# A decoder layer with a routed MoE on one core: the first weight half ahead of the second tile of x, and the second tile turned inside the first dense unit

## What is computed

```
h    = rmsnorm(x, g_mix)             # x * rsqrt(mean(x*x) + 1e-6) * g_mix
proj = h @ w_in                      # 1024 x 3848, q, k, v of two kinds of attention
...
gates = sigmoid(h @ w_gate + b_gate)
x     = x + merged @ w_out
...
x     = x + moe_ffn(rmsnorm(x, g_ffn))   # 64 experts, top 8, and a shared one
```

## Time and profile before

| | |
|---|---|
| median of 3 runs | 1102.56 us (1102.43 to 1103.54) |
| profiled execution, its own time | 1102.48 us |
| its span in the trace | 1100.7 us |
| TensorE busy | 1081.0 us, 98% |
| VectorE busy | 882.3 us, 80% |
| ScalarE busy | 739.3 us, 67% |
| GpSimd busy | 299.2 us, 27% |
| mean granted clock of TensorE | 0.997 of full speed |

### The profile page before, as it was taken

The page is one execution under the profiler, slowest core; times in us unless marked ns, Lnnn a source line. Parts: engine busy times, 40 slices in busy tenths (PEclk is TensorE's granted clock), DMA queues, the critical chain, the costliest instruction groups (busy, mean ns, idle before and its releaser), DMA issues.

```text
span 1100.7 us, 19484 instructions
## 1 busy us (share of the span) xinstructions
PE 1081.0 (98%) x5823; PEld 892.3 (81%) x5823; DVE 882.3 (80%) x1405; ACT 739.3 (67%) x1304; POOL 299.2 (27%) x288
## 2 busy tenths in 40 slices
PE   8999999999999999999999999999999999999995
PEld 7789988877777887678888888888888888888884
DVE  6543386478865835589999999999999999999993
ACT  6434465544346521268888888888888888888883
POOL 1221021000000001125433333344434444434442
PEclk9999999999999999999999999999999999999998
DMA  7243212421522093679999999999999999999982
GB/s 250 78 116 109 83 51 66 153 77 40 138 112 97 11 380 142 251 257 371 387 391 386 375 388 381 380 371 388 383 382 384 389 381 383 382 373 386 366 271 37
DMA packets 97353, 284.71 MB, mean 259 GB/s; under 512 B 19683, under 2 KB 22251, under 8 KB 96924
## 3 DMA queue, kind: packets, MB, share of 16 engines
q1 hardware_dynamic: 78876, 250.52, 59.6%
q0 software_dynamic: 18432, 33.61, 12.5%
HBM read 279.79 MB, written 37.81 MB: 289 GB/s over the span
## 4 chain that ended last, share of the span: by engine, by line
PE 91%; DVE 5%; ACT 1%; DMA 1%; issue 1%; POOL 1%; SPq 0%; ACTq 0%; POOLq 0%
PE bank L1849 32%; PE bank L1670 23%; PE bank L1863 17%; PE bank L1877 5%; PE bank L1823 3%; PE bank L1612 3%; PE bank L1837 3%; PE bank L1857 1%; DVE w_lo L1092 1%; PE bank L1697 1%; PE bank L1726 1%; PE bank L1739 1%; PE bank L1936 1%; PE bank L1715 1%; DMA arena<-in_x 0%
## 5 line engine op out<-in xcount | busy, mean ns | idle before, releaser
L1849 PE MATMUL bank<-gu_parts,xT_parts 128*128 128x512 f32 x1280 | 338.7, 394 | 0.0
L1849 PEld LDWEIGHTS bank<-gu_parts,xT_parts 128*128 128x128 f32 x1280 | 235.4, 188 | 45.9
L1863 PE MATMUL bank<-w_lo 128*128 128x512 f32 x804 | 201.6, 399 | 0.0
L1863 PEld LDWEIGHTS bank<-w_lo 128*128 128x128 f32 x804 | 146.3, 188 | 28.5 <-issue 0.5
L605 POOL TENSOR_TENSOR turn<-minus_half 16x1 f32<-16x1 f32 x123 | 73.6, 599 | 335.0 <-DMA out<-arena,idxs 174.4
L616 POOL DMA_INDIRECT out<-arena,idxs x64 | 124.7, 1948 | 46.0 <-issue 15.0
L1670 PE MATMUL bank<-w_hi,hT_hi 128*128 128x512 f32 (+1 forms) x320 | 124.8, 390 | 1.4 <-DVE arena L1187 0.7
L1670 PE MATMUL bank<-w_hi,hT_lo 128*128 128x512 f32 (+1 forms) x320 | 121.8, 381 | 0.0
L1670 PE MATMUL bank<-w_lo,hT_hi 128*128 128x512 f32 (+1 forms) x320 | 121.6, 380 | 0.0
L1452 DVE TENSOR_TENSOR gu_parts<-arena,gu_parts 128x1024 fp32r<-128x1024 f32 x96 | 116.6, 1215 | 0.4 <-PE bank L1837 0.3
L1452 DVE TENSOR_TENSOR gu_parts<-arena_x,gu_parts 128x1024 fp32r<-128x1024 f32 x96 | 116.6, 1215 | 0.1
(11 more groups left out here) (228 smaller groups left out, 1903.9 us busy)
## 6 DMA issues: line engine op xcount, KB each, us to landing
arena<-in_w_gate_e SPq DMA_DIRECT2D x64, 512.0 KB
arena<-in_w_up_e SPq DMA_DIRECT2D x64, 512.0 KB
arena<-in_w_down_e SPq DMA_DIRECT2D x64, 512.0 KB
arena_x<-in_w_gate_e SPq DMA_DIRECT2D x64, 512.0 KB
arena_x<-in_w_up_e SPq DMA_DIRECT2D x64, 512.0 KB
arena_x<-in_w_down_e SPq DMA_DIRECT2D x64, 512.0 KB
arena<-in_w_in SPq DMA_DIRECT2D x14, 1024.0 KB, 5.6
arena<-in_w_gate SPq DMA_DIRECT2D x8, 1024.0 KB, 5.6
```

The lines of the kernel that those rows point to most:

```text
L1849: last = nc.tensor.matmul(out_, a[:, PER * c + j, :], b[c][:, :, j, :], start=(c == 0 and j == 0 and i == 0), stop=(c == CHUNKS - 1 and j ...
L1863: last = nc.tensor.matmul(psY[h][0:rows, :], midT[n][a][:, j, 0:rows], w[b][:, j, h * 512:(h + 1) * 512], start=(j == 0 and k == 0), stop= ...
```

## The change

On SP, half 0 of chunk 0 is issued ahead of tile 1 of x, half 1 behind it. On ScalarE the square of tile 1 moves behind the high parts of blocks 0 to 3. On VectorE the copies and the low part of tile 0 and residues 0 to 3 come first; the mean of tile 1 follows, then residue 4, the scaling of tile 1, residues 5 and 6, the first copy of tile 1, residue 7, the second copy and the low part. On TensorE tile 1 is turned inside unit 0, after step 5, and the warm-up behind tile 0 is 56 products in one piece in place of 35 and 14.

```
--- before.py
+++ after.py
@@ -421,8 +421,9 @@
             load_x(0)
             sp.dma_start(cst[:], consts).then_inc(const_in, 16)
             sp.dma_start(gmixT[:], g_mix.rearrange("(p j) -> p j", p=P)).then_inc(const_in, 16)
+            load_half(0, 0)
             load_x(1)
-            load_chunk(0)
+            load_half(0, 1)
             for t in range(2, NT):
                 load_x(t)
             sp.dma_start(relb[0:REL_BUCKETS, :], rel_bias).then_inc(table_in, 16)
@@ -712,9 +713,11 @@
                 nc.scalar.activation(hT_hi[:, :, cols], hT[:, :, cols], ACT.Copy).then_inc(hT_hi_ready, 1)
 
             square_x(0)
+            high_hT(0)
+            for j in range(HALF):
+                split_block(0, j)
             square_x(1)
-            high_hT(0)
-            for j in range(ND):
+            for j in range(HALF, ND):
                 split_block(0, j)
             high_hT(1)
             square_x(2)
@@ -1107,22 +1110,22 @@
                 nc.vector.tensor_scalar(xn[t % 2], xin[t], hn_r[:, t:t + 1], None, ALU.mult).then_inc(xn_ready, 1)
 
             norm_x(0)
+            dve.wait_ge(const_in, 32)
+            copy_wide(("x", 0), hT, gmixT)
+            low_hT(0)
+            for j in range(HALF):
+                split_block(0, j)
             dve.wait_ge(squared, 2)
             means[0] += 1
             nc.vector.tensor_scalar(hn_ms[:, 1:2], hn_ss[:, 1:2], 1.0 / D, EPS, ALU.mult, ALU.add).then_inc(mean_ready, 1)
-            dve.wait_ge(const_in, 32)
-            copy_wide(("x", 0), hT, gmixT)
+            split_block(0, HALF)
             dve.wait_ge(rnorm_ready, means[0])
             nc.vector.tensor_scalar(xn[1], xin[1], hn_r[:, 1:2], None, ALU.mult).then_inc(xn_ready, 1)
-            low_hT(0)
-            for j in range(HALF):
-                split_block(0, j)
+            split_block(0, HALF + 1)
+            split_block(0, HALF + 2)
             copy_wide(("x", 1), hT, gmixT, (0,))
-            for j in range(HALF, HALF + 2):
-                split_block(0, j)
+            split_block(0, HALF + 3)
             copy_wide(("x", 1), hT, gmixT, (1,))
-            for j in range(HALF + 2, ND):
-                split_block(0, j)
             low_hT(1)
             norm_x(2)
             norm_x(3)
@@ -1636,9 +1639,7 @@
                     transposes(("x", t, b), [(xn[t % 2][:, j::ND], P) for j in range(b * ND // 2, (b + 1) * ND // 2)])
 
             turn_x(0)
-            keep_warm(WARM_UP * 5 // 8)
-            turn_x(1)
-            keep_warm(WARM_UP // 4)
+            keep_warm(WARM_UP)
             def stationary_of(h, j, t, by_residue):
 
                 return h[:, j, t::NT] if by_residue else h[:, j, t * P:(t + 1) * P]
@@ -1676,6 +1677,8 @@
             def dense(n):
                 for j in range(ND):
                     dense_step(n, j)
+                    if n == 0 and j == HALF + 1:
+                        turn_x(1)
                     if n == 1 and j in (2, 6):
                         turn_x(2 + j // 4)
```

## The result

| | before | changed |
|---|---|---|
| median of 7 runs each | 1103.45 us | 1106.64 us |
| lowest and highest | 1102.43 to 1104.07 | 1106.13 to 1108.60 |
| profiled execution, its own time | 1102.48 | 1108.60 |
| its span | 1100.7 | 1106.8 |
| ratio, 95% interval | | 1.0036 (1.0026 to 1.0045) |

The change makes the kernel slower by 0.36%, 2.9 to 5.0 us by the interval. The ratio goes by the means of the runs (1103.18 and 1107.13, 3.95 apart); the medians are 3.19 apart. The direction was forecast (slower, 0.73); the time of 1105.2 and the range up to 1106.3 were too low. Two things belong to that. The shift in the opening is 3.3 and not 2.75. And 1102.48, from which the sum started, lies 0.97 under the median of 1103.45, at the low end of what the kernel before does (1101.6 to 1105.9 in all its runs of this study).

A forecast was written before the change was run, and what follows sets the result against it. VectorE's program order was taken to bound the opening, TensorE the rest. Waits of 0.67, 0.67, 0.97 and 1.25 less 0.74 gave 2.8, taken as 2.75; on 1102.48 that made 1105.2 us, range 1103.9 to 1106.3.

The forecast's parts named there:

- The start: Opening: tile 0's copies no longer wait behind tile 1's mean, so dense work starts 0.74 us earlier, at 12.35.
- The four waits: VectorE in unit 0: half 1 0.67, scaling of tile 1 0.67, transposes 0.97, high part 1.25 us.
- The third: VectorE's wait for the transposes of tile 1 before its first copy, 0.97 us.
- the fourth: VectorE's wait for tile 1's high part, before the low part, 1.25 us.
- The first wait: VectorE before residue 4: half 1 lands at 14.0 as before, a new wait of 0.67 us.
- rival D: Opening loads: half 0, tile 1 or half 1 lands late; 3.1 to 3.8 us slower, 1105.6 to 1106.3; chance 0.06.
- The base: Whole kernel: the profiled execution's 1102.48 us, 0.08 under the median of three runs, to which the shift was added.
- The end: After the opening: every microsecond of TensorE's delay comes out at the end; 2.75 us added.
- A (absorbed): VectorE's chain holds less than added, above all at hand-overs; 0.8 us goes, 1104.4; chance 0.15.
- B (not slower): Low part of tile 1 ends by 19.6, VectorE's waits covered; 1102.5 us; chance 0.05.
- C (the clock): TensorE's clock falls to 1.2 GHz in unit 1; 5.5 us more, 1110.7; chance 0.04.
- the upper end of 10.9: Half 0 of chunk 0 lands at 10.9 as before instead of 9.2; 0.3 us more at the end.

The follow-up runs named there:

- copies_together: Changed kernel with both copies of tile 1 ahead of residue 7 instead of one on each side; 1106.40 us, ratio 1.0026 to the kernel before.
- loads_back: Changed kernel with the loads in their old order (tile 1 of x, half 0, half 1); 1106.47 us, ratio 1.0033 to the kernel before.
- loads_alone: Kernel before with only the new order of loads, every engine's list as before; 1107.47 us, ratio 1.0040.
- turn_and_copies: Changed kernel with tile 1 turned after step 4 and both its copies ahead of residue 7; 1104.55 us, ratio 1.0013 to the kernel before.
- delay: Kernel before with 56 more warm-up products on TensorE behind unit 3, opening untouched; 1106.74 us, ratio 1.0038.
- after_again: Changed kernel run once more, unaltered, for a second trace; 1107.27 us, ratio 1.0034 to the kernel before.

## Why the forecast was right, and where it failed

**The start.** Forecast: copies at 7.9, high part 9.28, low part 10.37, residue 0 at 11.51, first product 12.35. Measured: 7.92, 9.30, 10.39, 11.54, 12.37. The rule of start distances held to 0.03. Half 0 was forecast at 9.2 with 10.9 as the other end; it came at 9.5 and 10.65 in the two traces of the changed kernel, and 11.2 in copies_together, outside both ends. The warm-up products ended at 11.4, ahead of the first product, and cost nothing.

**The four waits.** Forecast 0.67, 0.67, 0.97 and 1.25; measured 1.11 (VectorE's mean at 13.94 to residue 4 at 15.05), 0.66 (15.66 to 16.32), 0.98 (from 17.53, when residue 6 lets go, to 18.51; the bracket, which counts from its modelled end, has 0.91) and 1.26 (20.33, when the second copy lets go, to 21.59). Three are right. The third was taken away whole and gave 0.99, and 0.60 of the fourth.

**The steps that failed** are two terms of the sum. The median of 1106.64 lies 1.44 over 1105.2: 0.97 of it is the base, 1102.48, and 0.44 the shift (3.19 between the medians, for 2.75). The mechanism was right. Set on 1103.45, the same sum gives 1106.2.

**The first wait:** "Then it waits for half 1, which lands at 14.0 as before". 14.0 was one landing. With the old order of issue half 1 was there at 13.96, 14.0, 14.0 (loads_back), 14.5 and 15.1, with the new one at 14.0 (loads_alone), 14.4, 14.5, 14.6, 14.8 and 15.1. Their mean is about 14.45, and the one that I had taken is among the earliest. This term was forecast at 0.67 and measured 1.11. Every figure after it, up to the scaling of the second unit's queries (forecast 37.7, measured 38.22), came 0.4 to 0.5 late, nearly all of it by this term. The means by order are 14.3 and 14.6: whether the new order itself delays half 1 by a few tenths, this many traces don't tell.

I did have the case, as rival D ("half 1 slips by half a microsecond"), and gave it 0.06. Of the eleven traces with these bytes ahead, six reach that half microsecond. The prediction held the answer to why it mattered: before, VectorE came to block 4 at 15.27, while it was ready at 14.59. These 0.7 were slack against a landing that scatters by 1.1. The change took the copy out from between, so the scatter goes straight into the low part: the distance from block 4 to it stayed within 7.18 to 7.21 while block 4 itself moved.

**The base.** The sum was set on 1102.48, and the three runs shown had their median next to it. With 7 runs the median was 1103.45, in later sets 1102.99, 1103.07, 1103.19, 1103.47 and 1102.55. So 1102.48 lies under all six, by 0.1 to 1.0, and against the runs made beside the changed kernel it was 0.97 too low. The prediction put nothing into its range for that.

**The end.** "1102.48 + 2.75" took the rest of the kernel as fixed. It is fixed up to 1000, not behind it. In the changed kernel's profile the last experts wait for weights, and the chain runs through the scatters from 963 on. The page's chain, and ScalarE's waits for transfers from 1000 on:

```profile
PE 79%; DMA 12%; DVE 4%; issue 1%; POOL 1%; ACT 1%; SPq 0%; POOLq 0%; ACTq 0%
```

```profile
ACT gu_parts L969 <- DMA arena<-in_w_up_e: 2.8, 2, 1.5
ACT gu_parts L969 <- DMA arena_x<-in_w_up_e: 0.9, 1, 0.9
```

TensorE's share of the chain was 91% in the earlier trace rows. The second trace of the unchanged kernel has the same kind of rows:

```profile
PE 76%; DMA 14%; DVE 5%; issue 2%; POOL 1%; ACT 1%; POOLq 0%; SPq 0%; ACTq 0%
```

```profile
ACT gu_parts L966 <- DMA arena<-in_w_up_e: 1.9, 2, 1.0
```

So it is not made by the change. The chain's share of transfers is no measure of what the end adds: in turn_and_copies, which added 1.7, it is small.

```profile
PE 89%; DVE 5%; DMA 2%; ACT 2%; issue 1%; POOL 1%; SPq 0%; ACTq 0%; DVEq 0%; POOLq 0%
```

ScalarE's waits go with it better. From 1000 on it waits for transfers (weights and scatters) 3.7 to 6.7 us in the four traces that add 1.0 or more, and 0 to 2.6 in the ten others; no run took these waits away. In eight traces of kernels that are late by 1.9 or more at 930, the end adds 0.85 on average (0 to 2.05), in the six others 0.3 (0 to 1.0). Whether a late kernel really pays more there, or whether this is chance, stays open: the ratio of the delay run, 2.5 to 5.7 us for a shift of 3.26, allows both. It matters for the size in the time (3.2 by the medians, 4.0 by the means) against 3.3 in the opening, not for its sign.

**The rivals.** A (absorbed): nothing was; the two slack waits of TensorE stayed, as said. B (not slower): the low part ended at 22.8, 3.2 behind the 19.6 that this rival asked for. C (the clock): 1.00 in all of the first 40 us, also in the stretch with 1.3 us of idle in 5. That it can fall in this opening is seen in loads_alone, after a wait of 4.04.

On the rule of the Trainium skill, "DMA: Bandwidth & Descriptors", section "Queues, rings and completion order", that completion is not first in, first out: tile 1 and the two halves landed in their order of issue in every trace, so the upper end of 10.9 was not reached by a turned order. Further back in the same queue the order was turned round, as the rule says: in the changed kernel's first trace tile 3 of x, issued at 4.21, landed 13.4 later, at 17.6, and a transfer of 0.2 KB (`in_q_norm_a`), issued at 6.47, landed 9.7 later, at 16.2. For the moment of a landing the place in the queue is a weak guide: half 0 came on average at 11.0 with tile 1 ahead of it and at 10.3 without, 0.7 earlier for the 1.7 forecast, and with one and the same order of issue it came between 9.5 and 11.2.

## What to carry to other kernels

One trace gives one landing of each transfer. Where a change takes away the work that stood between a landing and its user, price the scatter and not the landing: here a half that came 1.1 late cost 0.16 in the old list, and in the new one a half 0.43 late cost all of it. The same holds for the base of a sum: one execution is one draw. When an operation moves into a pipeline, look for what is left between it and its user on each engine: the transposes themselves took 0.8, but the copy that waited for them and the high part with nothing beside it cost 0.9 and 1.3. And where the time scatters by more than the edit is worth, the distance between two instructions in the trace still tells what the edit did.

## What the runs showed of the hardware

The landing of a 1 MB weight half, behind 2.4 MB in the same queue, scattered from 10.8 to 12.0 us after its issue over the eleven traces with these bytes ahead, and half 0, behind 0.8 MB, from 7.4 to 9.1 over the six with the new order. The compute engines' start distances did not scatter: from block 4 to the low part of tile 1 were 7.20, 7.21 and 7.18 us in three executions. I had treated both as equally firm; the first scatters by 1.2, the second by 0.03. The chip does not explain it: three traces taken on one chip (loads_alone, after_again, delay) span the whole range, 10.8, 11.4 and 12.0.

Waits of TensorE of up to 1.5 us in the openings left its granted clock at 1.00, the level of 2.4 GHz. After the one of 4.04 in loads_alone it was 0.50, the level of 1.2 GHz, from 15 to 17, and 1.00 again from 18 on. In that stretch eight transposes took 1.97 us in place of 1.16.
